# The odd layer's gates and latents moved beside its input projection, norms by token tile, weight splits ahead of them

## What is computed

```python
# first block, for l in 0, 1:
h = rms_norm(x, g_norm_mix[l]) * (1 + sc1) + sh1
mix = mixers(h @ w_in[l]) @ w_out[l]
x = x + g1 * mix
h = rms_norm(x, g_norm_ffn[l]) * (1 + sc2) + sh2
x = x + g2 * (swiglu(h) if l == 0 else moe_swiglu(h))    # 8 experts, top 2
x = rms_norm(x, g_final)
# second block, for layer in 0, 1:
h = rmsnorm(x, norm_mix_g[layer])
x = x + (even_mixer(h) if layer == 0 else odd_mixer(h))
mem_n = rmsnorm(mem, mem_norm_g[layer])
x = x + memory_cross_attention(rmsnorm(x, norm_xattn_g[layer]), mem_n)
x = x + swiglu_2(rmsnorm(x, norm_ffn_g[layer]))
# odd_mixer
q_m, k_m, v_m, o_m, gates, c_q, c_kv, k_r = split(h @ w_in)      # 512 x 4, 8, 384, 256, 32 columns
hm = rmsnorm(sigmoid(o_m) * mlstm(q_m, k_m, v_m, gates + gate_bias))   # 4 heads of 128
q, kv = rmsnorm(c_q) @ w_uq, rmsnorm(c_kv) @ w_ukv               # latents to heads
ha = causal attention of q, kv with rope                          # 8 heads
return concat(hm, ha) @ w_out
```

## Time and profile before

| | |
|---|---|
| runs, us | 2709.71, 2707.74, 2710.9 (median 2709.71) |
| profiled execution, its own time | 2713.55 us |
| its span, first to last instruction | 2711.8 us |
| instructions | 30606 |
| busy: TensorE, DVE, ACT, POOL | 85%, 69%, 49%, 2% |
| DMA: bytes, mean rate | 595.17 MB, 219 GB/s |
| MoE stage (745 to 1800 us) | 334 to 347 GB/s |
| the second block begins at | 1815 us |

### The profile page before, as it was taken

The page is one execution under the profiler, slowest core; times in us unless marked ns, Lnnn a source line. Parts: engine busy times, 40 slices in busy tenths (PEclk is TensorE's granted clock), DMA queues, the critical chain, the costliest instruction groups (busy, mean ns, idle before and its releaser), DMA issues.

```text
span 2711.8 us, 30606 instructions
## 1 busy us (share of the span) xinstructions
PE 2311.4 (85%) x11133; PEld 1903.6 (70%) x11133; DVE 1857.9 (69%) x1948; ACT 1337.1 (49%) x1425; POOL 41.9 (2%) x102
## 2 busy tenths in 40 slices
PE   4836899875699999999999999966869988486998
PEld 4725688764578787878777787756758877475786
DVE  7776676777488887888788888865454443644543
ACT  2412333342367776777677777742344433333442
POOL 1000000000000000000000000000000000000000
PEclk9856999895799999999999999988989998688999
DMA  8730578640179999999999999963315553131453
GB/s 300 274 124 1 193 273 305 211 155 0 47 257 347 337 347 319 348 342 345 313 343 347 345 345 330 359 222 124 124 59 175 186 186 105 63 106 65 144 186 128
DMA packets 412855, 595.17 MB, mean 219 GB/s; under 512 B 20315, under 2 KB 326726, under 8 KB 412742
## 3 DMA queue, kind: packets, MB, share of 16 engines
q1 hardware_dynamic: 407040, 586.55, 62.7%
q10 hardware_dynamic: 5702, 7.04, 0.8%
HBM read 592.47 MB, written 1.05 MB: 219 GB/s over the span
## 4 chain that ended last, share of the span: by engine, by line
PE 61%; DVE 6%; DMA 3%; ACT 3%; issue 2%; POOL 0%; SPq 0%; DVEq 0%; ACTq 0%
PE bank L136 18%; PE bank L137 18%; PE bank L138 18%; DMA ring<-in_moe_w_up 2%; PE bank L2351 1%; PE bank L2370 1%; DVE ring_rounded L645 1%; PE bank L2330 1%; PE bank L461 1%; DVE ring_rounded L287 1%; PE bank L1143 1%; ACT PT_rounded L278 1%; ACT xn L386 0%; PE bank L1681 0%; DVE xn L423 0%
## 5 line engine op out<-in xcount | busy, mean ns | idle before, releaser
L136 PE MATMUL bank<-ring_rounded,hT_rounded 128*128 128x512 f32 (+3 forms) x944 | 377.7, 400 | 48.5 <-DVE ring_rounded L287 45.7
L645 DVE TENSOR_TENSOR ring_rounded<-ring,zT_rounded 128x2048 fp32r<-128x2048 f32 x147 | 336.9, 2292 | 51.8 <-ACT zT_rounded L637 49.9
L136 PE MATMUL bank<-ring_rounded,z_rounded 128*128 128x512 f32 x896 | 363.1, 405 | 10.1 <-issue 6.8
L645 DVE TENSOR_TENSOR ring_rounded<-ring,z_rounded 128x2048 fp32r<-128x2048 f32 x143 | 327.7, 2292 | 61.8 <-ACT z_rounded L637 60.1
L136 PE MATMUL bank<-ring_rounded,L_rounded 128*128 128x512 f32 x712 | 286.7, 403 | 16.7 <-DVE score_rounded L778 11.1
L637 ACT ACTIVATE zT_rounded<-ring 128x2048 fp32r<-128x2048 f32 x147 | 281.6, 1916 | 33.6 <-DMA ring<-in_moe_w_up 20.7
L637 ACT ACTIVATE z_rounded<-ring 128x2048 fp32r<-128x2048 f32 x143 | 274.2, 1917 | 39.2 <-DMA ring<-in_moe_w_up 25.1
L136 PEld LDWEIGHTS bank<-ring_rounded,hT_rounded 128*128 128x128 f32 x944 | 183.5, 194 | 87.5 <-issue 52.7
L136 PEld LDWEIGHTS bank<-ring_rounded,z_rounded 128*128 128x128 f32 x896 | 169.4, 189 | 49.5 <-issue 9.5
L645 DVE TENSOR_TENSOR ring_rounded<-ring,PT_rounded 128x2048 fp32r<-128x2048 f32 x74 | 169.5, 2290 | 42.1 <-ACT PT_rounded L637 41.8
L645 DVE TENSOR_TENSOR ring_rounded<-ring,mix_rounded 128x2048 fp32r<-128x2048 f32 x71 | 162.6, 2290 | 29.9 <-ACT mix_rounded L637 29.0
(11 more groups left out here) (479 smaller groups left out, 5079.8 us busy)
## 6 DMA issues: line engine op xcount, KB each, us to landing
ring<-in_moe_w_gate SPq DMA_DIRECT2D x224, 512.0 KB, 5.2
ring<-in_moe_w_up SPq DMA_DIRECT2D x224, 512.0 KB, 7.2
ring<-in_moe_w_down SPq DMA_DIRECT2D x224, 512.0 KB, 7.9
ring<-in_ffn_w_gate_up SPq DMA_DIRECT2D x88, 512.0 KB, 4.9
ring<-in_ffn_w_down SPq DMA_DIRECT2D x66, 512.0 KB, 7.8
ring<-in_w_ada SPq DMA_DIRECT2D x48, 512.0 KB, 7.0
ring<-in_w_in SPq DMA_DIRECT2D x32, 512.0 KB, 4.7
xn<-in_w_ada SPq DMA_DIRECT2D x24, 512.0 KB, 9.6
```

The costliest lines, as they stand in the source:

```text
L136: pe.matmul(out, r32(a[0]), r32(b[1]), start=start, stop=False, skip_group_check=True)
L645: dve.tensor_tensor(r32(w), w, high(hi[slot]), ALU.subtract).then_inc(sem_out, 1)
```

## The change

It does four things.

1. **The odd layer.** The tiles of `od_in` come in another order: columns 2048 to 2388 (gates and most of c_q) and 2388 to 2728 (the rest of the latents) first, then q and k, then v, o. The stages `mlstm` and `mla_in` are cut into pieces that hang as `fill`s between the tiles of `od_in` and of `latents` on each engine (a new ('pe', i) fill stands before tile i). The last step of mLSTM, scaling by its norm, stands ahead of the attention on DVE. The latents' high half is made by ACT, straight from PSUM, the low half by one DVE operation a chunk.
2. **Norms by token tile.** `x_ready` counts token tiles. Squares, POOL, scaling and transposes go tile by tile (all chunks of token tile 0, then those of tile 1). The final norms do the same, and the gain row is asked for one update of x earlier.
3. **Splits ahead.** Where the stage before a norm is a projection or an FFN (and the stage behind it not the MoE), the first two splits of the next weights move ahead of the last evacuation (in an FFN: the first ahead of both evacuations on DVE, the second behind them). For that the high buffers get another order, `od_out` and the other output projections have four instead of six, and `hi_free` waits for a buffer's last reader.
4. **Norms beside projections.** The memory norms and the cross-attention norms are `beside` the projection before them: squares and scaling before its last evacuation, transposes before its last tile.

```diff
@@ proj_pe
-    for tl in st['tiles']:
+    for ti, tl in enumerate(st['tiles']):
+        if tl is st['tiles'][-1] and st['then'] and st['then']['beside']:
+            norm_turn_pe(c, pe, st['then'])
+        if ('pe', ti) in st['fill']:
+            st['fill']['pe', ti](pe)
@@ proj_act
+    if st['then']:
+        if st['then']['beside']:
+            norm_squares_act(c, act, st['then'])
+        early_splits(c, act, st['then'])
     evacuate(before)
@@ proj_dve
-    evacuate(before)
-    if before['evac'] != 'copy':
-
-        dve.wait_ge(c.s['proj_evac_b'], before['t'] + 1)
-        c.x_written(dve)
+    if st['then']:
+        if st['then']['beside']:
+            norm_scale_dve(c, dve, st['then'])
+        early_splits(c, dve, st['then'])
+    evacuate(before, True)
@@ norm_act
+    if st['early'] == 'ffn':
+        early_splits(c, act, st)
+    if not st['beside']:
+        norm_squares_act(c, act, st)
...
-    for i in range(2):
-        first_split(c, act, st['next'], i)
+    if not st['early']:
+        early_splits(c, act, st)
@@ norm_pool
-    pool.wait_ge(c.s['norm_ss'], NT * k + NT)
-    c.pstep(pool.tensor_scalar(c.ms[:, 0:NT], c.ss[:, 0:NT], 1.0 / D, EPS, ALU.mult, ALU.add))
-    pool.tensor_tensor(c.rstd[:, 0:NT], c.ms[:, 0:NT], c.neghalf[:, 0:NT], ALU.pow)\
-        .then_inc(c.s['rstd_ready'], 1)
+    for n in range(NT):
+        pool.wait_ge(c.s['norm_ss'], NT * k + n + 1)
+        c.pstep(pool.tensor_scalar(c.ms[:, n:n + 1], c.ss[:, n:n + 1], 1.0 / D, EPS, ALU.mult, ALU.add))
+        pool.tensor_tensor(c.rstd[:, n:n + 1], c.ms[:, n:n + 1], c.neghalf[:, 0:1], ALU.pow)\
+            .then_inc(c.s['norm_rstd'], 1)
@@ norm_pe, now norm_turn_pe
+    for n in range(NT):
+        pe.wait_ge(c.s['norm_xn'], NT * k + n + 1)
+        for j in range(4):
+            for i in range(2):
                 kc = 2 * j + i
                 mm = pe.transpose(c.pb[j][:, i * S + n * P:i * S + n * P + P],
                                   c.xn[:, n, kc * P:kc * P + P], c.ident[:, :])
-        mm.then_inc(c.s['norm_turned'], 1)
+            if n == NT - 1:
+                mm.then_inc(c.s['norm_turned'], 1)
@@ ffn_dve, behind the loop
+    if st['then']:
+        first_split(c, dve, st['then']['next'], 0)
     for n in range(NT):
...
-    c.x_written(dve)
+        c.x_written(dve)
+    if st['then']:
+        first_split(c, dve, st['then']['next'], 1)
@@ mlstm and mla_in, now pieces of these names
+def odd_fill(c, p, la):
+    def logs(act):
+        mla_squares_act(c, act, p)
+        mlstm_log_act(c, act)
+    def scans(dve):
+        mlstm_scan_dve(c, dve)
+        mla_norm_dve(c, dve, la)
+    def turn(pe):
+        mla_turn_pe(c, pe)
+        mlstm_cols_pe(c, pe)
+    def columns(dve):
+        mlstm_cols_dve(c, dve)
+        mla_low_dve(c, dve)
+    def gates(dve):
+        tile_evacuated(c, dve, p, 0)
+        mlstm_gates_dve(c, dve)
+    return {('dve', 1): gates, ('pe', 2): lambda pe: mlstm_rows_pe(c, pe),
+            ('dve', 2): lambda dve: mlstm_abs_dve(c, dve), ('act', 2): logs, ('dve', 3): scans, ('pe', 4): turn,
+            ('act', 4): lambda act: mla_high_act(c, act), ('dve', 4): columns,
+            ('pe', 5): lambda pe: mlstm_spread_pe(c, pe, p), ('act', 5): lambda act: mlstm_exp_act(c, act),
+            ('dve', 5): lambda dve: mlstm_exponent_dve(c, dve)}
+def latents_fill(c, p):
+    return {('pe', 0): lambda pe: mlstm_last_scores_pe(c, pe), ('dve', 0): lambda dve: mlstm_weigh_dve(c, dve, 2),
+            ('act', 0): lambda act: mlstm_sigmoid_act(c, act, p), ('pe', 1): lambda pe: mlstm_num_pe(c, pe, p),
+            ('dve', 2): lambda dve: mlstm_out_dve(c, dve), ('act', 3): lambda act: mlstm_square_act(c, act),
+            ('dve', 3): lambda dve: mlstm_sums_dve(c, dve)}
@@ mla_dve
     mla_evacuate(c, dve, 1)
+    mlstm_mix_dve(c, dve, st['mlstm'])
     attend_dve(c, dve, st['att'])
@@ make_plan
-            p = add(proj(c, 'od_in', c.hsplit, [], feat(v, 0, 1024, 0) + tok(v, 1024, 2728, dst), c.hi_in, h))
-            add(dict(kind='mlstm', evacuated=proj_evacuated(p)))
-            add(dict(kind='mla_in', evacuated=proj_evacuated(p)))
+            p = add(proj(c, 'od_in', c.hsplit, [], tok(v, 2048, 2388, z(1024)) + tok(v, 2388, 2728, z(1364)) +
+                         feat(v, 0, 1024, 0) + tok(v, 1024, 1536, z(OD_V)) + tok(v, 1536, 2048, z(OD_O)), c.hi_in, h))
+            la, ml = add(dict(kind='mla_in')), add(dict(kind='mlstm'))
+            p['fill'] = odd_fill(c, p, la)
...
-            p = add(proj(c, 'latents', (c.rT, c.hL), [('la_ready', 1)],
+            p = add(proj(c, 'latents', (c.rT, c.laL), [('la_ready', 1), ('proj_done', 2 * od['tiles'][-1]['t'] + 2)],
@@ build
+        c.hi_in, c.hi_kv = [PTf, mixf, Lf], [Lf, PTf, mixf]
+        c.hi_latent = [PTf, Lf[:, 0:SLOT // 2], Lf[:, SLOT // 2:SLOT]]
+        c.hi_out = [PTf, zT0, zT1, mixf]
+        c.hi_ffn = [z0, z1, zT0, PTf, mixf, zT1]
```

359 lines of the change are left out of this document (218 added, 141 removed).

## The result

The changed kernel took 2673.69 us (median of 5 executions, 2661.47 to 2674.45) against 2709.71 before: ratio 0.985, with a 95% interval from 0.9831 to 0.9869. Five more executions beside the experiments gave 2666.29 (2662.62 to 2674.52) against 2710.26, ratio 0.985 again (0.9827 to 0.9874). All ten together have their middle at 2670.3. The gain is about 40 us where I had forecast 50.9 in the sum; the forecast of 2660 stands 6 to 14 us too low, inside its range.

What follows compares the result with a forecast made beforehand. TensorE, busy 85% of the span, bounds the kernel, so its waits can be won: 35.6 + 4.4 + 2.4 + 3.0 - 1.8 + 0.5 + 5.6 + 1.2 = 50.9 us off 2713.55 gives 2662.6 (2658.8 against the median); forecast 2660, range 2649 to 2680.

Steps and rivals of the forecast that it cites:

- hole in the odd layer: Between odd input projection and latents' projection: 48.5 us of gates, mLSTM and latent norms, TensorE working 20.1 of them.
- the second rival: Odd projection: late fills in DVE and ACT queues push weight splits into TensorE's way, 6 to 22 us, 2666 to 2682; chance 0.17.
- the tightest place: Odd projection, before tile 3: first weight's split ready at 26.1 us, needed at 27.0, so 0.9 us of cover.
- Odd layer: Odd projection to attention: rotations start at 89.4 us instead of 125.6; gain 35.6 us, bounds 20 to 39.
- The 0.6 us for the mixing steps: Odd layer: mixing steps (2.8 us on DVE) stand ahead of the first attention maximum, where DVE waited 2.2; 0.6 lost.
- My first rival: Odd layer: clock falls at the new 2.4 us pauses, slowing latents and numerators by 4 to 10 us, 2664 to 2670; chance 0.13.
- First seam and FFN: First gated output projection to dense FFN: hT 2.4 us earlier and a 2.27 us low-half wait gone; together 4.4 gained.
- FFN to projection: FFN to input projection: early low halves delay x; 1.8 us lost in the first block, 0.5 gained in the odd layer.
- Cross-attention to FFN: Cross-attention output to FFN, twice: first product at 2016.4 instead of 2017.6; with the clock 1.5 us each, 3.0 gained.
- The third rival: Splits ahead hold up x at five seams and POOL; all seam gains but the final norms' go (-9.7), 2670; chance 0.09.
- Final norms and the seam to the MoE: Final norms, twice: 2.8 us gained each, 5.6; second gated projection to the MoE: 2.4 gained.
- Norms beside a projection: Memory and cross-attention norms, two each: shorter gaps almost offset by stops before the last tile; 1.2 us gained together.

Runs made afterwards that it cites:

- mended order: Changed kernel with latents' split ahead, mLSTM output later, low halves behind scalings after FFNs, only the first ahead after cross-attention: 2650.89 us, 0.9777 of the kernel before.
- unchanged order: The changed kernel as first measured, no further edit: 2673.69 us, then 2666.29 us in five more executions; ratio 0.985 to the kernel before.

## Why the prediction was partly right

**The mechanism and the sign were right.** The hole in the odd layer closed as told: no stretch over 4 us with TensorE idle, no wait inside the projection (the second rival, cover failing, did not come), numerators at 5.27 us for 5.2, the wait before the latents' last tile 2.29 for 2.4. ACT's work in the tightest place also ran as the rows of before had it: two table loads of 1.28 us, the next activation 0.01 us behind each (the first load at 2222.77, its activation at 2224.06). The extra drain of the Trainium skill (ScalarE: Activation LUTs, What ACT_TABLE_LOAD costs) did not show. The 0.9 us of cover held: tile 3's low half was ready at 2230.33 and first used at 2231.18.

**Odd layer, 35.6 forecast, 29.2 to 29.9 seen.** The rotations were to start at 89.4 us and started at 95.6. Step by step: the projection took 68.2 instead of 65.6; the first two tiles alone 17.2 instead of 14.9 at a mean clock of 0.86. The latents' first tile 5.8 instead of 4.1, tiles one and two 5.15 instead of 4.9, the last 4.6 instead of 2.8. The same two tiles take 4.35 and 3.00 where the clock holds, so of the 6.2 us some 5.3 are clock (2.3, 1.4, 1.6) and 0.9 are paces that I had put too low. The runs that fill or remove the pauses show this for the two tiles of the latents; the 2.3 us of the projection's first tiles are worked out from their mean clock. The order of work was right; the failed step is the price, which took all products at the upper clock. The 0.6 us for the mixing steps did not come: from rotation to output projection it is 42.96 before and 42.98 after. My first rival had this mechanism (4 to 10 us, chance 0.13) and came true in the latents, at 3.0 us and not 4 to 10, since the numerators stayed at the upper clock; the projection's first tiles it didn't name. I had set its weight by one pause of 2.70 us that fell and one that didn't, and argued that 2.4 is shorter than both. It's no argument: the clock fell behind 2.28 us in 11 of 13 places. And the pause of 2.70 us that didn't cool (2444.6) did in the second profile of the same kernel.

**First seam and FFN, 4.4 forecast, 2.4 and 2 to 3 seen.** The seam is exact. The wait of 2.27 us in the earlier trace rows is gone: the FFN's length less the time lost to the lower clock goes from 202.8 and 203.2 to 201.2 and 199.9. Of the 8.8 us in the profiled pair 1.6 are this and 7.1 are clock, 5 of them behind one-column products. No step of mine had the clock in this stage, and it is what made the profiled execution meet the sum.

**FFN to projection, 1.8 lost forecast, 2.8 seen.** x came complete 3.3 us later (forecast 3.5). The step that failed is the next: I let the norm by token tile win 0.9 back, and overlooked that the second low half stands ahead of the first scaling in DVE's queue and beside POOL's second power. With both low halves put elsewhere the seam is 5.0 us shorter. In the odd layer 0.5 was forecast and 0.8 seen, but the projection behind began at a lower clock, and the mended order gets 1.7 more.

**Cross-attention to FFN, 1.5 each forecast, 1.48 and 1.48 seen, and about half of it given back.** The sum ended at the FFN's first product. Its next 8 us went from a clock of 0.88 to 0.75, and the FFNs took 191.6 and 191.5 to 192.2 instead of 190.6 to 191.3 and 190.8: 0.6 and 1.0 us by the means of two profiles. The third rival had "splits ahead cost more, all seam gains go" at 2670; the total it gives is what was measured, but by another road, since the seams did shorten.

**Final norms and the seam to the MoE** came as forecast (2.7 to 3.1 and 3.1 for 2.8; 2.45 for 2.4).

**Norms beside a projection, 1.2 forecast, 0.1 to 1.7 seen.** Stops and gaps are as costed (3.4 and 2.7 for 3.5 and 2.8; 3.2 and 2.0 for 3.6 and 2.0). What I missed is the comparison: once the norm goes by token tile with early splits, the plain gap is 5.1 and 4.8 and not 6.4 and 5.8, so "beside" loses 2.3 to 3.4 us a layer against not doing it (3.4 in the unchanged order, 2.3 and 3.3 in the mended one). Parts of one change were costed against the kernel before, and not against the other parts.

Together: 6.1 in the odd layer, 1.0 behind the first FFN, 1.6 in the later FFNs' first products; less some 0.8 that the other parts brought beyond their forecasts. That is 8 of the 10 us. The other 2 are within what unedited stages move by, and stay open. The stages can't be read closer than that: the two pairs of profiled executions differ by 52.0 and 43.1 us, the two pairs of medians by 36 and 44.

## What to carry to other kernels

A seam is not over with the first product behind it: look at the granted clock of the next 8 us before you book its gain, and compare the stage, not the seam. Cost each part of a change against the kernel with the other parts in, and walk each engine's queue from the moved instruction to the next thing that someone waits for; here two subtractions of 2.3 us, in the wrong place at the seam behind the first FFN, cost 5.0 us, more than the norm by token tile won at any seam. And compare a profile with a second profile of the same kernel, stage by stage, before a stage's difference is explained.

## What the runs showed of the hardware

TensorE's clock fell to 0.50 while the engine was counted busy all the time, behind 32 one-column products in 3.6 to 4.4 us (six of the eight groups in the first FFN of the four profiles of the two kernels, 15 of 24 in all twelve profiles with such rows), and not when the same products stood among full ones (four of four). They weren't its only place there: in several profiles it also fell some 22 us behind the second row, behind a pause of about 2 us. Pauses of 2.28 us were followed by 3 to 4 us at the lower level in 11 of 13 places; for one program going both ways there is the pause of 2.70 us at 2444.6 in the kernel before, behind which the clock held in one execution and fell in the other. Whether the clock is up when work resumes can be worth more than a change of the seam: before the later FFNs the mended kernel saves 0.8 us in the seam and, where the clock held, 1.2 to 2.5 us behind it. With the same seam it didn't hold in one of the three profiles.
